# The first FFN chunk of a two-layer encoder: input in four parts, and products of both tiles by k-step

## The reference

```python
def rms_norm(x, g):
    y = x * rsqrt(mean(x * x, axis=-1) + 1e-6)
    return y * g

def swiglu(h, w_gate, w_up, w_down):          # w_gate, w_up: 1024 x 2816, w_down: 2816 x 1024
    return (silu(h @ w_gate) * (h @ w_up)) @ w_down

for l in range(2):
    x = x + 0.5 * swiglu(rms_norm(x, ffn1_norm[l]), ffn1_w_gate[l], ffn1_w_up[l], ffn1_w_down[l])
    h = rms_norm(x, mix_norm[l]); z = h @ w_in[l]
    x = x + concat([attention(z[q, k, v]), pool(z[p])]) @ w_out[l]
    x = x + 0.5 * swiglu(rms_norm(x, ffn2_norm[l]), ffn2_w_gate[l], ffn2_w_up[l], ffn2_w_down[l])
out = rms_norm(x, final_norm)
```

## Time and profile before

| | |
|---|---|
| median of 3 runs | 940.3 us (940.12 to 941.12) |
| profiled execution | 941.15 us, span 939.0 us |
| TensorE busy | 927.4 us, 99% of the span |
| VectorE busy | 551.0 us, 59% |
| ScalarE busy | 499.4 us, 53% |
| transfers | 174.66 MB, mean 186 GB/s |

### The profile page before, as it was taken

The page is one execution under the profiler, slowest core; times in us unless marked ns, Lnnn a source line. Parts: engine busy times, 40 slices in busy tenths (PEclk is TensorE's granted clock), DMA queues, the critical chain, the costliest instruction groups (busy, mean ns, idle before and its releaser), DMA issues.

```text
span 939.0 us, 12733 instructions
## 1 busy us (share of the span) xinstructions
PE 927.4 (99%) x4299; PEld 759.0 (81%) x4299; DVE 551.0 (59%) x896; ACT 499.4 (53%) x821; POOL 44.1 (5%) x81
## 2 busy tenths in 40 slices
PE   8999999999999999999999999999999999999996
PEld 6888888887778888888888888888877888888885
DVE  4655465558756655556476455465786565554654
ACT  5654454557636545545465455454675474544542
POOL 1010100010001001001010000000100000000000
PEclk9999999999999999999999999999999999999998
DMA  7867778855245777776465657556444276465531
GB/s 231 297 163 205 216 166 235 290 174 210 90 135 168 203 219 200 183 235 174 119 231 197 207 194 249 196 168 202 135 151 151 64 264 211 146 222 179 177 136 45
DMA packets 123532, 174.66 MB, mean 186 GB/s; under 512 B 8384, under 2 KB 99696, under 8 KB 123248
## 3 DMA queue, kind: packets, MB, share of 16 engines
q1 hardware_dynamic: 117744, 165.70, 52.7%
q0 software_dynamic: 2848, 6.38, 5.8%
q10 hardware_dynamic: 2912, 2.22, 0.7%
HBM read 173.14 MB, written 4.19 MB: 189 GB/s over the span
## 4 chain that ended last, share of the span: by engine, by line
PE 97%; DVE 1%; ACT 1%; issue 1%; POOL 0%; POOLq 0%; DVEq 0%
PE ps L987 30%; PE ps L990 29%; PE ps L988 29%; PE ps L1084 2%; PE ps L998 1%; PE ps L997 1%; PE ps L1198 1%; PE ps L1072 1%; PE ps L1214 1%; PE ps L1226 1%; PE ps L1242 1%; DVE xt_lo L744 1%; PE ps L1047 0%; ACT xt_hi L490 0%; PE ps L1335 0%
## 5 line engine op out<-in xcount | busy, mean ns | idle before, releaser
L987 PE MATMUL ps<-w_hi,xt_hi 128*128 128x512 f32 x856 | 342.0, 400 | 2.6 <-DVE w_lo L730 1.3
L988 PE MATMUL ps<-w_lo,xt_hi 128*128 128x512 f32 x856 | 334.3, 390 | 0.0
L990 PE MATMUL ps<-w_hi,xt_lo 128*128 128x512 f32 x856 | 329.7, 391 | 0.0
L730 DVE SCALAR_TENSOR_TENSOR w_lo<-w_raw,gains,w_hi 128x512 fp32r<-128x512 f32 x416 | 284.7, 747 | 76.3 <-ACT w_hi L475 75.3
L475 ACT ACTIVATE w_hi<-w_raw,gains 128x512 fp32r<-128x512 f32 x408 | 260.8, 713 | 73.9 <-PE ps L990 73.7
L721 DVE TENSOR_TENSOR w_lo<-w_raw,w_hi 128x1024 fp32r<-128x1024 f32 x104 | 122.7, 1222 | 123.9 <-ACT w_hi L468 123.8
L987 PEld LDWEIGHTS ps<-w_hi,xt_hi 128*128 128x128 f32 x856 | 161.2, 188 | 40.8 <-issue 4.0
L990 PEld LDWEIGHTS ps<-w_hi,xt_lo 128*128 128x128 f32 x856 | 161.0, 188 | 34.7
L988 PEld LDWEIGHTS ps<-w_lo,xt_hi 128*128 128x128 f32 x856 | 161.4, 189 | 30.6
L468 ACT ACTIVATE w_hi<-w_raw 128x1024 fp32r<-128x1024 f32 x104 | 104.4, 1052 | 116.3 <-PE ps L990 116.3
L987 PE MATMUL ps<-w_hi,gt_hi 128*128 128x512 f32 x352 | 138.0, 392 | 0.0
(11 more groups left out here) (84 smaller groups left out, 405.1 us busy)
## 6 DMA issues: line engine op xcount, KB each, us to landing
w_raw<-in_ffn_w_down_dram SPq DMA_DIRECT2D x88, 512.0 KB, 4.3
w_raw<-in_ffn_w_gate_dram SPq DMA_DIRECT2D x86, 512.0 KB, 4.0
w_raw<-in_ffn_w_up_dram SPq DMA_DIRECT2D x86, 512.0 KB, 5.1
w_raw<-in_w_in_dram SPq DMA_DIRECT2D x32, 512.0 KB, 4.8
w_raw<-in_w_out_dram SPq DMA_DIRECT2D x16, 512.0 KB, 5.2
bias_scratch<-in_rpb_dram POOLq DMA_DIRECT2D x32, 96.0 KB, 6.1
bias<-bias_scratch POOLq DMA_DIRECT2D x2, 1536.0 KB, 7.1
pool_m<-in_pool_matrix_dram ACTq DMA_DIRECT2D x1, 1024.0 KB, 9.4
```

The lines of the kernel that those rows point to most:

```text
L730: nc.vector.scalar_tensor_tensor(w_lo[slot][:, part], w_raw[slot][:, part], g, w_hi[slot][:, part].bitcast(F32), ALU.mult, ALU.subtract).t ...
L987: nc.tensor.matmul(o, hi, wh, start=start, stop=False)
L988: nc.tensor.matmul(o, hi, wl, start=False, stop=False)
L990: last = nc.tensor.matmul(o, lo, wh, start=False, stop=bool(stop))
```

## The change

- `load_first`: x comes in four parts (tile and half). The order is x(0,0), gate and up of quarter 0, x(1,0), quarters 1 to 3, x(0,1), x(1,1), and then slot 1 in two parts.
- Tile 1 is transposed into accumulator banks (`xt_bank`: banks 4 and 5), in all stages, and its transposes no longer wait for `xt_lo_ready` of tile 0.
- `first_gate_up`: slot 0's k-steps run for both tiles in the order (k, t) = (0,0), (1,0), (0,1), (1,1), (2,0), (2,1), (3,0), (3,1). The first two matmuls of a step wait only for `w_hi` (and `xt_lo`), the third for `w_lo`. The transposes of x(1,0) stand within step (0,0), those of x(0,1) behind step (2,1), those of x(1,1) and of the other gains behind step (3,1). Slot 1 follows tile by tile.
- The order of `store_xt_hi` and `store_xt_lo` follows: (0,0), (1,0), (0,1), (1,1).
- Six warm-up products instead of eight, and two more (`FILL`) behind the first transposes.
- ScalarE loads its activation table ahead of the loads of the second and third gains.

```diff
--- before.py
+++ after.py
@@ -50,7 +50,8 @@
 SLOTS = 3
 DELTAS = ROWS + 2
 STAGES = 3
-WARM_UP = 8
+WARM_UP = 6
+FILL = 2
 GATHER_FROM = 2
 PAGE_PAD = 480
 
@@ -158,6 +159,15 @@
 
 
 
+        def xt_bank(t, h):
+            return acc(1, h) if t == 1 else ps[:, 6 + h, :]
+
+        def first_weights(weights, a, m, k0, k1):
+
+            dst = w_raw[FF1["g"][a]][:, :].rearrange("p (k m c) -> p k m c", k=4, m=2)
+            src = weights[m][0, a * 512 + k0 * P:a * 512 + k1 * P, 0:FC]
+            return dst[:, k0:k1, m, :], src.rearrange("(k p) c -> p k c", p=P)
+
         def diff_t(g):
             return z[:, g // 2, 1, (g % 2) * SEQ:(g % 2 + 1) * SEQ]
 
@@ -172,8 +182,7 @@
         first_raw = [sem(f"first_raw{q}") for q in range(6)]
         ident_loaded = sem("ident_loaded")
         tables_loaded = sem("tables_loaded")
-        x_loaded = [sem(f"x_loaded{t}") for t in range(TT)]
-        x_half_loaded = sem("x_half_loaded")
+        x_loaded = [[sem(f"x_loaded{t}{h}") for h in range(2)] for t in range(TT)]
         bias_rows_loaded = sem("bias_rows_loaded")
         gains_loaded = [sem(f"gains_loaded{j}") for j in range(STAGES)]
         gains_t_ready = sem("gains_t_ready")
@@ -242,6 +251,10 @@
 
             return layer * (2 * N_FF_CHUNKS) + ((ff["stage"] // 2) * N_FF_CHUNKS + i)
 
+        def xt_no(number, t, h):
+
+            return number * 4 + (2 * h + t if number == 0 else 2 * t + h)
+
         def first_unit(layer, ff, a):
 
             return ff["g"][a], unit_no(layer, ff["stage"], ff["g"][a], 0)
@@ -280,24 +293,28 @@
                     sp.dma_start(dst[:, kt, :], src.rearrange("o p c -> p (o c)")
                                  ).then_inc(raw_ready[slot], 16)
 
-            def load_first(layer, ff, weights):
-
-                def quarter(a, k0, k1, q):
-                    slot = ff["g"][a]
-                    dst = w_raw[slot][:, :].rearrange("p (k m c) -> p k m c", k=4, m=2)
-                    for m, w in enumerate(weights[:2]):
-                        src = w[layer, a * 512 + k0 * P:a * 512 + k1 * P, 0:FC]
-                        sp.dma_start(dst[:, k0:k1, m, :], src.rearrange("(k p) c -> p k c", p=P)
-                                     ).then_inc(first_raw[q], 16)
-
-                sp.dma_start(resid[:, 0, 0:512], x[0, 0:P, 0:512]).then_inc(x_half_loaded, 16)
-                quarter(0, 0, 1, 0)
-                sp.dma_start(resid[:, 0, 512:], x[0, 0:P, 512:]).then_inc(x_loaded[0], 16)
-                for k in range(1, 4):
-                    quarter(0, k, k + 1, k)
-                sp.dma_start(resid[:, 1, :], x[0, P:2 * P, :]).then_inc(x_loaded[1], 16)
-                quarter(1, 0, 2, 4)
-                quarter(1, 2, 4, 5)
+            def load_first(weights):
+
+                def x_half(t, h):
+                    part = slice(h * BANK, (h + 1) * BANK)
+                    sp.dma_start(resid[:, t, part], x[0, t * P:(t + 1) * P, part]
+                                 ).then_inc(x_loaded[t][h], 16)
+
+                def first_half(a, m, k0, k1, q):
+                    dst, src = first_weights(weights, a, m, k0, k1)
+                    sp.dma_start(dst, src).then_inc(first_raw[q], 16)
+
+                x_half(0, 0)
+                for k in range(4):
+                    for m in range(2):
+                        first_half(0, m, k, k + 1, k)
+                    if k == 0:
+                        x_half(1, 0)
+                for t in range(TT):
+                    x_half(t, 1)
+                for q in (4, 5):
+                    for m in range(2):
+                        first_half(1, m, 2 * (q - 4), 2 * (q - 3), q)
 
             def load_ff(layer, ff, weights, begun=0):
                 for i in range(begun, 2):
@@ -429,10 +446,10 @@
 
             load_gain(0)
             act.dma_start(ident[:, :], identity).then_inc(ident_loaded, 16)
+            act.wait_ge(eps_ready, 1)
+            nc.scalar.activation(table_seed[:, :], eps[:, :], ACT.Silu)
             for j in (1, 2):
                 load_gain(j)
-            act.wait_ge(eps_ready, 1)
-            nc.scalar.activation(table_seed[:, :], eps[:, :], ACT.Silu)
 
             def load_params(layer):
                 act.dma_start(w_pool_sb[:, :, :], w_pool[layer, :, :, :].rearrange("g c d -> c g d")
@@ -477,17 +494,16 @@
 
             def squares(number, t):
                 if number == 0:
-                    act.wait_ge(x_loaded[t], 16)
-                    if t == 0:
-                        act.wait_ge(x_half_loaded, 16)
+                    for h in range(2):
+                        act.wait_ge(x_loaded[t][h], 16)
                 else:
                     act.wait_ge(resid_ready[t], 2 * number)
                 nc.scalar.activation(normed[:, t, :], resid[:, t, :], ACT.Square,
                                      scale=D_MODEL ** -0.5, accum_out=mean_sq[:, t:t + 1]).then_inc(sq_ready[t], 1)
 
             def store_xt_hi(number, t, h):
-                act.wait_ge(xt_ready, number * 4 + (2 * t + h + 1))
-                nc.scalar.activation(xt_hi[:, t, 4 * h:4 * h + 4, :], ps[:, 6 + h, :],
+                act.wait_ge(xt_ready, xt_no(number, t, h) + 1)
+                nc.scalar.activation(xt_hi[:, t, 4 * h:4 * h + 4, :], xt_bank(t, h),
                                      ACT.Copy).then_inc(xt_hi_ready, 1)
 
             def norm(layer, stage, late, late_used):
@@ -515,11 +531,11 @@
                 act.wait_ge(gains_stored, 1)
                 for k in range(2):
                     first_hi(k, 0, k)
-                store_xt_hi(0, 0, 1)
+                store_xt_hi(0, 1, 0)
                 for k in range(2, 4):
                     first_hi(k, 0, k)
-                for h in range(2):
-                    store_xt_hi(0, 1, h)
+                for t in range(TT):
+                    store_xt_hi(0, t, 1)
                 squares(0, 0)
                 for k in range(4):
                     first_hi(4 + k // 2, 1, k)
@@ -766,10 +782,10 @@
                 slots = FF1["g"]
                 store_xt_lo(0, 0, 0)
                 split_lo(slots[0], 0, gains_of=(0, 0, 0), halves=(0,))
-                store_xt_lo(0, 0, 1)
+                store_xt_lo(0, 1, 0)
                 split_lo(slots[0], 0, gains_of=(0, 0, 0), halves=(1,))
-                for h in range(2):
-                    store_xt_lo(0, 1, h)
+                for t in range(TT):
+                    store_xt_lo(0, t, 1)
                 split_lo(slots[1], 0, gains_of=(0, 0, 4))
 
             def gate(layer, ff, i, t):
@@ -1058,20 +1074,20 @@
                                       [w_hi[slot][:, c] for c in cols],
                                       [w_lo[slot][:, c] for c in cols], start, stop)
 
+            def transpose_half(number, t, h):
+                if number == 0:
+                    pe.wait_ge(x_loaded[t][h], 16)
+                else:
+                    pe.wait_ge(resid_ready[t], number * 2 + (h - 1))
+                for k in range(4):
+                    c = (4 * h + k) * P
+                    last = nc.tensor.transpose(xt_bank(t, h)[:, k * P:(k + 1) * P],
+                                               resid[:, t, c:c + P], ident[:, :])
+                last.then_inc(xt_ready, 1)
+
             def transpose_resid(number, t):
                 for h in range(2):
-                    if number == 0:
-                        pe.wait_ge(*((x_half_loaded, 16) if (t, h) == (0, 0) else (x_loaded[t], 16)))
-                    else:
-                        pe.wait_ge(resid_ready[t], number * 2 + (h - 1))
-                    if t == 1:
-
-                        pe.wait_ge(xt_lo_ready, number * 4 + (h + 1))
-                    for k in range(4):
-                        c = (4 * h + k) * P
-                        last = nc.tensor.transpose(ps[:, 6 + h, k * P:(k + 1) * P],
-                                                   resid[:, t, c:c + P], ident[:, :])
-                    last.then_inc(xt_ready, 1)
+                    transpose_half(number, t, h)
 
             def gate_up(layer, ff, i, t, before={}):
                 numbers = [unit_no(layer, ff["stage"], s, i) for s in ff["g"]]
@@ -1102,24 +1118,46 @@
 
             def first_gate_up():
 
-                for a in range(2):
-                    slot = FF1["g"][a]
+                slot = FF1["g"][0]
+
+                def first_step(k, t):
+
+                    cols = slice(k * BANK, (k + 1) * BANK)
+                    pe.wait_ge(hi_ready[slot], k + 1)
+                    if k == 0:
+                        pe.wait_ge(xt_lo_ready, xt_no(0, t, 0) + 1)
+                    nc.tensor.matmul(ps[:, t, :], xt_hi[:, t, k, :], w_hi[slot][:, cols],
+                                     start=k == 0, stop=False)
+                    nc.tensor.matmul(ps[:, t, :], xt_lo[:, t, k, :], w_hi[slot][:, cols],
+                                     start=False, stop=False)
+                    if (k, t) == (0, 0):
+                        transpose_half(0, 1, 0)
```

(46 more changed lines are left out.)

6 lines of the change are left out of this document (3 added, 3 removed).

## The result

The changed kernel takes 943.19 us, the median of 11 runs (942.42 to 944.32); the kernel before takes 940.45 us in 11 runs (940.12 to 941.12), 0.15 more than in the three runs that the forecast was counted from. The ratio is 1.0029, with a 95% interval of 1.0021 to 1.0036: slower by 2.7 us. That is outside the forecast range (939.0 to 942.8), above it.

A forecast was written before the change was run, and what follows sets the result against it. TensorE, busy for 927.4 of 939.0 us, was taken as the bound, with only the time before 20 us able to move. The late second-slot reload's net +0.7 us on the 940.3 median gave 941.0 us; range 939.0 to 942.8.

The forecast's parts named there:

- What bounds the kernel: Whole kernel: TensorE is busy for 927.4 of 939.0 us; all that can move lies before 20 us and in the tail.
- the later stages at 0: Stages after the first chunk: new banks and the dropped wait taken at 0, at most 0.2 us of gain.
- Start of the first chunk: First chunk: first product at 6.7 instead of 8.14, 1.4 us gained; tile 1's first product at 9.35 after 0.7 us idle.
- The middle, at full clock: First chunk from 9.35: last transposes behind 24 products instead of 12; last xt_hi at 14.57 instead of 13.72, 0.85 us later.
- What is queued behind that xt_hi: Squares and second slot's splits shift by 0.85 us; TensorE idles 2.7 us until 17.6; the chunk ends 0.1 us later.
- The transfer behind it: Second slot's next load shifts by 0.85 us against 0.15 of slack; TensorE starts at 26.4 instead of 25.68, net +0.7 us.
- Rival 2: Low clock early, the 12 products from 9.35 slow: last xt_hi at 15.9, net +2.0, 942.3 to 943.2 us; chance 0.16.
- Rival 1: Second slow stretch of the clock after the 2.7 us idle before 17.6: net +1.5, 941.8 us; chance 0.24.
- Rival 3: First chunk: TensorE never idles, last xt_hi and slot release 1.0 us earlier; net -1.1, 939.2 us; chance 0.15.

The follow-up runs named there:

- b1: The kernel before with only tile 1 transposed into two accumulator banks in all stages, without the wait for tile 0's low part; 940.67 us, ratio 0.9999.
- e2: The changed kernel with the second slot's splits moved ahead of the waits for x's second halves on ScalarE and VectorE; 940.55 us, ratio 0.9996.
- e3: The changed kernel with the last four transposes of x moved from behind k-step 3 to behind k-step 2; 940.95 us, ratio 1.0005.
- e4: The changed kernel with ScalarE's squares of tile 0 moved behind the second slot's four w_hi; 942.15 us, ratio 1.0017.
- e7: e2 with both squares moved ahead of the second slot's splits, into ScalarE's idle time; 939.30 us, ratio 0.9987.
- e9: The changed kernel with five fill products behind the first transposes instead of two; 943.55 us, ratio 1.0035.
- e10: The changed kernel with TensorE's product order undone: tile 0's four k-steps, both last sets of transposes, then tile 1's four; 940.05 us, ratio 0.9995.

## Why the prediction was wrong

The direction of the time was forecast right (+0.7), its size too small by a factor of four. The step that failed is the clock at the start. The forecast ran the changed kernel at full clock from its first transposes on and laid it beside a trace of before that was partly at the low clock; so the last xt_hi was to move by 0.85 us, and it moved by 2.02 to 2.39. Point by point:

- **What bounds the kernel; the later stages at 0.** Right: b1 is at 0.9999, and all of the difference is there by 31 us.
- **Start of the first chunk.** Here the size failed first: tile 1's first product came at 10.79 instead of 9.35, 1.44 us late. The transposes started at 4.54 (forecast 4.44), but ran at the low clock: xt_hi stood 1.15 us behind their start, at 5.69 instead of 5.15, where the forecast took 0.7 from the trace of before (e2's and e3's traces have 0.69). That made the first product 0.54 us late (7.24, forecast 6.7). From it to tile 1's first product the forecast had 2.65 us, and e2, e4, e7 and e9, at full clock there, have 2.64; the changed kernel's trace has 3.55. So 0.9 us is the clock between 7.2 and 10.8, some 0.45 the clock in the first transposes, and 0.1 their later start. The second w_hi did wait for its weights until 7.49 instead of 6.75, but set nothing: the xt_hi behind it, at 9.32, waited for transposes.
- **"The middle, at full clock".** The way from tile 1's first product to the last xt_hi was right: 5.32 us (forecast 14.57 - 9.35 = 5.22). What failed here is the other side of the comparison: the trace of before had the low stretch, so seven slow products counted as won. Whether the clock is low there differs between executions of either kernel. Like beside like, the last xt_hi moves by 2.39 us (both partly low: 16.11 - 13.72) or 2.02 us (both full: 15.15 in e4, which is the changed kernel up to there, against b1's 13.13), not by 0.85.
- **What is queued behind that xt_hi.** Right in mechanism, and within 0.3 us in size once the start is given: first w_hi of the second slot 1.53 us behind the last xt_hi (17.64 - 16.11; forecast 16.1 - 14.57), idle time 2.98 (forecast 2.7). e10, e2, e3 and e4 touch this queue alone or what it waits for, and each gives back all or part of the loss.
- **The transfer behind it.** Right: reload at 21.15, w_hi at 26.56 behind its transfer, w_lo at 27.31, TensorE at 28.12. The net is 28.12 - 25.68 = 2.44 us, instead of 26.4 - 25.68 = 0.7.
- **Rival 2** is the nearest to the traced execution: last xt_hi at 15.9, net +2.0, 942.3 to 943.2; measured 16.11, +2.44, 943.19. Its mechanism holds, a low clock early on that never rose in the warm-up; its place does not. It had the 12 products from 9.35 slow; in the trace those ran at full clock, from 10.79, and the transposes and products ahead of them were slow. That the sizes agree is in part luck. What was wrong was its chance, 0.16. The reason given against it, that TensorE had more to do ahead of 8.8 us, did not keep the clock up in the execution traced.
- **Rival 1** was seen once, in e3's profiled execution (0.52 behind an idle time of 1.65 us), not in that of the changed kernel, where the idle time was 2.98 us. By the mean granted clocks it is likely in most of the untraced runs (9 of the 11), and its chance of 0.24 was probably too low as well. **Rival 3** failed: even at full clock tile 1's first product waited for its xt_lo (0.58 us in e4's trace), as was held against it.

How much of the 2.7 us in the median is clock is known only roughly. The early low stretch is 1 us at most by the traces (31.01 against e9's 30.05). For the low stretch that most runs have on record, an estimate from the times is 0.8 to 1.0 us: the one untraced run of the changed kernel at 0.999 took 942.42 us and the nine at 0.995 or 0.996 have 943.19 as their median; in e9 it is 942.54 at 0.997 against 943.45 and more. That leaves 1.7 to 1.9 us for the order itself, and it fits what e3 and e4 gained: 1.4 and 0.2 us of shift, and 0.8 each besides. Where that stretch lay in those runs stays open.

## What to carry to other kernels

Ask of each instruction that is pushed back not only who waits for it but what stands behind its consumer in a queue that keeps its order: here four transposes behind twelve more products held up 1 us of squares, four splits, and through a buffer's release a 5 us transfer. Putting work that has its data (the squares, the splits) ahead of a wait won back 3.9 us (943.19 to 939.30), of which some 0.8 is likely a clock that no longer falls. And before two kernels are compared by a trace, compare the pace of like instructions in both: a slow stretch in the one trace that is shown may be that execution's, not the kernel's.

## What the runs showed of the hardware

The clock at the start differs between executions of the same instructions. Up to tile 1's first product the TensorE programs of the changed kernel, e2, e3 and e4 are the same; it came at 10.79, 9.61, 10.39 and 9.87. The first four transposes took 0.69 us to the engine behind them in the traces of before, e2 and e3, and 1.15 in those of the changed kernel and e4. The windows read 1.00 through the changed kernel's low stretch and 0.50 in e3's from 8 to 10 us. Three more fill products (e9) or two more warm-up products (e1) brought no gain in the median. With an idle time of 2.98 or 2.99 us in the first chunk 18 of 23 runs have a mean granted clock of 0.996 or less, with 0.57 or 1.23 us (e7, e2) none of 22.
